# Moving eight modulation pairs of a diffusion backbone's opening from TensorE to VectorE, with split constants

## The reference

```python
ada_x = (silu(c) @ w_ada[l] + b_ada[l]).reshape(1, 1, 6, D)      # w_ada: (2, 1024, 6144)
ada_c = (silu(c_ctx) @ w_ada[l] + b_ada[l]).reshape(1, 1, 6, D)
h  = rms_norm(x, g1[l]) * (1 + ada_x[1]) + ada_x[0]
x  = x + ada_x[2] * mixer(h)          # l = 0: gated conv || spatial-gating MLP; l = 1: conformer || attention
h2 = rms_norm(x, g2[l]) * (1 + ada_x[4]) + ada_x[3]
x  = x + ada_x[5] * peer(h2)          # query, top-k search over keys, gather of 128 expert rows per token
```

## Time and profile before

| | us |
|---|---|
| median of 3 runs | 2404.74 (2398.95 to 2406.70) |
| profiled execution, its time | 2403.09 |
| profiled execution, its span | 2401.3 |

### The profile page before, as it was taken

The page is one execution under the profiler, slowest core; times in us unless marked ns, Lnnn a source line. Parts: engine busy times, 40 slices in busy tenths (PEclk is TensorE's granted clock), DMA queues, the critical chain, the costliest instruction groups (busy, mean ns, idle before and its releaser), DMA issues.

```text
span 2401.3 us, 24278 instructions
## 1 busy us (share of the span) xinstructions
PE 2093.0 (87%) x7016; PEld 1120.0 (47%) x7016; DVE 1550.1 (65%) x3844; ACT 958.4 (40%) x2802; POOL 1017.8 (42%) x868
## 2 busy tenths in 40 slices
PE   6997998789999988988799899798799987777777
PEld 4775554345566534543355355335456532222222
DVE  1126658885765577778856866854665887666444
ACT  2113434454333444444454333534443444444333
POOL 0002444444334454444545444430233555566774
PEclk9999999999999999999999999998899999999999
DMA  9966999999999999999999999995599999999997
GB/s 405 414 228 275 383 418 421 421 422 416 414 398 400 410 422 420 421 421 421 419 421 419 415 409 420 408 334 227 201 379 387 415 421 422 421 421 421 422 419 318
DMA packets 132451, 939.44 MB, mean 391 GB/s; under 512 B 14704, under 2 KB 17776, under 8 KB 18672
## 3 DMA queue, kind: packets, MB, share of 16 engines
q0 software_dynamic: 110592, 805.36, 81.7%
q1 hardware_dynamic: 21744, 132.68, 13.7%
HBM read 936.93 MB, written 1.05 MB: 391 GB/s over the span
## 4 chain that ended last, share of the span: by engine, by line
PE 35%; DMA 20%; DVE 10%; issue 5%; POOL 5%; ACT 4%; POOLq 0%; SPq 0%; DVEq 0%; ACTq 0%
DMA uv<-uv_dram,stage_idx 20%; PE psum L868 20%; PE psum L682 7%; DVE uv L1449 5%; POOL uv L936 5%; PE psum L664 4%; PE psum L813 1%; ACT diag L1107 1%; ACT wv L1105 1%; ACT gel L1103 0%; PE psum L842 0%; DVE work L1413 0%; PE psum L608 0%; DMA wring<-ada_dram 0%; PE psum L775 0%
## 5 line engine op out<-in xcount | busy, mean ns | idle before, releaser
L868 PE MATMUL psum<-uv,diag 128*128 128x512 f32 x3072 | 1452.9, 613 | 245.0 <-ACT diag L1107 238.2
L936 POOL DMA_INDIRECT uv<-uv_dram,stage_idx x768 | 981.6, 1278 | 1067.2 <-PE psum L868 834.4
L1449 DVE CUSTOM_DVE_ANT_0 uv<-uv,h 128x1024 f32<-128x1024 f32 x768 | 933.0, 1226 | 462.5 <-DMA uv<-uv_dram,stage_idx 451.7
L868 PEld LDWEIGHTS psum<-uv,diag 128*128 128x128 f32 x3072 | 561.7, 193 | 1032.6 <-ACT diag L1107 515.5
L1103 ACT ACTIVATE gel<-dots 128x1 f32<-128x1 f32 x768 | 154.5, 201 | 933.9 <-DVE dots L1449 931.5
L1107 ACT ACTIVATE diag<-const,wv 128x128 f32<-128x128 f32 x768 | 308.4, 402 | 25.0
L682 PE MATMUL psum<-hT,wring 128*128 128x256 f32 (+1 forms) x1344 | 284.6, 366 | 1.5 <-ACT hT L977 1.5
L682 PEld LDWEIGHTS psum<-hT,wring 128*128 128x128 f32 x1344 | 242.7, 194 | 63.3 <-issue 35.4
L1105 ACT ACTIVATE wv<-gel,gw 128x1 f32<-128x1 f32 x768 | 226.2, 295 | 24.9
L922 POOL COPY stage_idx<-idx 128x8 uint32 (+1 forms) x96 | 36.1, 376 | 293.3 <-DVE idx L1421 292.7
L959 ACT ACTIVATE work<-psum 128x256 f32<-128x256 f32 (+2 forms) x122 | 48.7, 400 | 251.6 <-PE psum L682 195.4
(11 more groups left out here) (210 smaller groups left out, 1284.7 us busy)
## 6 DMA issues: line engine op xcount, KB each, us to landing
uv<-ada_dram SPq DMA_DIRECT2D x37, 1024.0 KB, 12.7
wring<-in_dram SPq DMA_DIRECT2D x25, 1024.0 KB, 9.1
wring<-wq_dram SPq DMA_DIRECT2D x24, 1024.0 KB, 11.6
uv<-uv_dram,stage_idx POOLq DMA_INDIRECT x768
wring<-ada_dram SPq DMA_DIRECT2D x11, 1024.0 KB, 7.0
uv<-in_dram SPq DMA_DIRECT2D x9, 1024.0 KB, 16.7
wring<-out_w_dram SPq DMA_DIRECT2D x5, 1024.0 KB, 8.9
wring<-out_dram SPq DMA_DIRECT2D x4, 1024.0 KB, 11.1
```

The lines of the kernel that those rows point to most:

```text
L868: last = mm(acc[:, b, :], diag[:, s % RING, :], uv[:, s % RING, D + 512 * b:D + 512 * (b + 1)], start=(c == 0), stop=(c == NSEL - 1))
L936: nc.gpsimd.indirect_dma_start(out=uv[:, s, :], out_offset=None, in_=tables[stage // 2], in_offset=bass.IndirectOffsetOnAxis(ap=stage_idx[ ...
L1449: v.tensor_tensor_reduce(out=uv[:, r, 0:D], in0=uv[:, r, 0:D], in1=h2[:, row_of[stage], t, :], scale=1.0, scalar=0.0, op0=ALU.mult, op1=AL ...
```

## The change

Eight of the pairs of the opening (10 and 11 of layer 0, 0 to 5 of layer 1) are no longer computed by TensorE. Their weights come transposed (`ada_t`: a block holds two chunks, 128 partitions x 2 x 1024), and VectorE multiplies each chunk by the row of silu(c) and by that of silu(c_ctx), with the sum written to `ada_c` (a new step `ada_row`, 32 of them, two instructions each), and adds the bias after each fourth. The c rows are the vectors repeated on all partitions (1.05 MB, a new transfer), put through Silu by ScalarE at the first `mods`. `ada_row` steps are dealt among the steps of `project_even`, `gate` and `out_rows`; then the eight pairs left on TensorE (4 to 9 of layer 0, 6 and 7 of layer 1) among all of these. The constants come in two transfers: 276 columns first, the rest ahead of block 9. The scaling of x stands ahead of the wait for the modulation. TensorE does 28 products of ones ahead of everything, 14 and 6 more ahead of pairs 2 and 3, whose results nobody reads. The v projection of a tile waits for that tile of hT alone. Blocks up to the last dealt step are 54 in both kernels.

```diff
+ADA_ROWS = ((0, 10, 12), (1, 0, 6))
-PARTS = [("ident", P), ("iota", TOPK), ("cos", TT * 32), ("sin", TT * 32), ("c", KC * 2), ("b_ada", 2 * 48),
+PARTS = [("ident", P), ("c", KC * 2), ("b_ada", 2 * 48), ("norm_g", 2 * 2 * KC), ("gather_sums", 4),
+         ("iota", TOPK), ("cos", TT * 32), ("sin", TT * 32), ...
+W_EARLY = AT["iota"][0]
...
-        0: ada(0, 0, 2) + rms(0)[:3] + ada(0, 2, 4) + [("mods", 0, 0)] + rms(0)[3:] + norm(0, 0)
-        + deal(project_even(0), ada(0, 4, 12) + ada(1, 0, 4)) + gate(0, 0) + deal(out_rows(0, 0), ada(1, 4, 8)) + [("mods", 0, 1)]
+        0: [("idle", 28)] + ada(0, 0, 2) + rms(0) + [("idle", 14)] + ada(0, 2, 3)[:1] + [("idle", 6)] + ada(0, 2, 4)[1:] + [("mods", 0, 0)]
+        + norm(0, 0)
+        + deal(deal(project_even(0) + gate(0, 0) + out_rows(0, 0), [s for layer, first, last in ADA_ROWS for s in ada_rows_of(layer, first, last)]),
+               ada(0, 4, 10) + ada(1, 6, 8)) + [("mods", 0, 1)]
...
+            def idle(n_products):
+                for _ in range(n_products):
+                    mm(psum[:, 7, 0:P], ones[:, :], ones[:, :], start=True, stop=True)
...
             def v_project(stage, b, t):
-                wait_hT()
+                wait_hT(("hT", t))
...
-            sp.dma_start(const[:, :], A["const"]).then_inc(const_loaded, 16)
+            sp.dma_start(const[:, 0:W_EARLY], A["const"][:, 0:W_EARLY]).then_inc(const_loaded, 16)
...
+                if n == 9:
+                    sp.dma_start(const[:, W_EARLY:], A["const"][:, W_EARLY:]).then_inc(tables_loaded, 16)
+                if n == 9:
+                    sp.dma_start(c_rows[:, :, :], A["c_rows"]).then_inc(c_rows_loaded, 16)
...
             def mods(stage, which):                                   # ScalarE
-                n.up("mods")
+                if n.up("mods") == 1:
+                    act.wait_ge(c_rows_loaded, 16)
+                    f(c_rows, c_rows, ACT.Silu).then_inc(c_rows_ready, 1)
...
+            def ada_row(layer, chunk):                                # VectorE
+                i = n.up("ada_row") - 1
+                k = row_blocks[i // 2]
+                if i == 0:
+                    dve.wait_ge(c_rows_ready, 1)
+                dve.wait_ge(w_landed[w_slot[k]], landed[k])
+                if i:
+                    dve.wait_ge(row_sums, 2 * i)
+                w = w_home(k).rearrange("p (c d) -> p c d", c=2)[:, chunk % 2, :]
+                for j in range(2):
+                    v.tensor_tensor_reduce(out=row_tmp[:, j, :], in0=w, in1=c_rows[:, j, :], scale=1.0, scalar=0.0, op0=ALU.mult,
+                                           op1=ALU.add, accum_out=ada_c[:, layer, chunk, j:j + 1]).then_inc(row_sums, 1)
+                if chunk % 4 == 3:
+                    dve.wait_ge(row_sums, 2 * i + 2)
+                    pair = ada_c[:, layer, chunk - 3:chunk + 1, :]
+                    bias = C("b_ada", 2, 48)[:, layer, chunk - 3:chunk + 1].unsqueeze(2).to_broadcast([P, 4, 2])
+                    v.tensor_tensor(pair, pair, bias, ALU.add).then_inc(row_pairs, 1)
```

More of the change, by code:

```diff
@@ L97, in ada, with ada_rows_of @@
     return out + [("ada_turn", layer, last - 1)]
+def ada_rows_of(layer, first, last):
+    return [("ada_row", layer, chunk) for chunk in range(4 * first, 4 * last)]
 def gate(stage, which):
@@ L266, in weight_blocks @@
             uses = [(("ada", args[0], 2 * args[1] + j), ("ada", args[0], 2 * args[1] + j)) for j in range(2)]
+        elif name == "ada_row":
+            uses = [(("ada_row", args[0], args[1] // 2), ("ada_t", args[0], args[1] // 2))]
         elif name == "out_half":
@@ L438, in build @@
         row_of = (0, 1, 1)
+        c_rows = h2[:, 0, :, :]
+        row_tmp = h2[:, 1, :, :]
         kept_sc = vx[:, :, :].rearrange("p a (b c) -> p (a b) c", c=2 * PK).rearrange("p h (q k) -> p h q k", q=2)
@@ L462, in build @@
         const_loaded, x_loaded, ctx_loaded = sem("const_loaded"), sem("x_loaded"), sem("ctx_loaded")
-        constants_set = sem("constants_set")
+        tables_loaded, constants_set = sem("tables_loaded"), sem("constants_set")
         w_landed = [sem(f"w_landed{i}") for i in range(WRING + RING)]
@@ L470, in build @@
         dve_chain = sem("dve_chain")
+        c_rows_loaded, c_rows_ready, row_sums, row_pairs = (sem(s) for s in ("c_rows_loaded", "c_rows_ready", "row_sums", "row_pairs"))
         silu_ready, mods_ready, gdiag_ready = sem("silu_ready"), sem("mods_ready"), sem("gdiag_ready")
@@ L502, in build @@
         left = [{w_slot[k] - WRING: k for k in range(len(blocks)) if w_slot[k] >= WRING and in_gap[k] == g} for g in (False, True)]
+        landed = [16 * w_slot[:k + 1].count(w_slot[k]) for k in range(len(blocks))]
+        row_blocks = [k for k in range(len(blocks)) if blocks[k][0] == "ada_t"]
         def w_home(k):
@@ L577, in _ @@
         def _(pe):
-            n = Tally()
+            n = Tally(block=0)
             to_act, to_dve = act_banks(), dve_banks()
@@ L584, in weights @@
             def weights(what):
+                while n["block"] in row_blocks:
+                    n.up("block")
                 k = n.up("block") - 1
-                pe.wait_ge(w_landed[w_slot[k]], 16 * n.up(("w_slot", w_slot[k])))
+                pe.wait_ge(w_landed[w_slot[k]], landed[k])
                 held[what] = (k, w_home(k))
@@ L627, in ada_turn @@
                 taken["ada", layer, pair] = (act_took, to_act.n)
+            def ada_row(layer, chunk):
+                if chunk % 2:
+                    done = n.up("row_block")
+                    multiplied[row_blocks[done - 1]] = (row_sums, 4 * done)
+                if chunk % 4 == 3:
+                    taken["ada", layer, chunk // 4] = (row_pairs, n.up("row_pair"))
             def gate(stage, which, half):
@@ L637, in gate, with turn_rows @@
                 taken["gate", stage, which] = (act_took, to_act.n)
-            def turn_rows(*_):
+            def turn_rows(*args):
                 k = n.up("xn_ready")
@@ L649, in turn_rows, with wait_hT @@
                     banks.fill(last)
[L650 to L655, removed]
+                n["hT"] = n["hT", args[-1]] = (to_act.n, to_dve.n)
+            def wait_hT(of="hT"):
+                pe.wait_ge(act_took, n[of][0])
+                pe.wait_ge(dve_took, n[of][1])
             def token_major(banks, src, what, new, done):
@@ L848, in score @@
                     taken["scores", k, t] = (act_took, to_act.n)
-            steps = {"ada": ada_pair, "ada_turn": ada_turn, "gate": gate, "norm": turn_rows, "norm_ctx": turn_rows,
+            steps = {"idle": idle, "ada": ada_pair, "ada_turn": ada_turn, "ada_row": ada_row, "gate": gate, "norm": turn_rows, "norm_ctx": turn_rows,
                      "v_rows": v_project, "u_cols": noted("u_cols"), "ah_cols": noted("ah_cols"), "cg_cols": noted("cg_cols"),
@@ L874, in _ @@
             pe.wait_ge(constants_set, 1)
-            pe.wait_ge(const_loaded, 16)
             walk(steps, nothing, add_values, nothing)
@@ L1041, in conv_out_step @@
             def conv_out_step(stage):
+                act.wait_ge(tables_loaded, 16)
                 act.wait_ge(cn_ready, 1)
@@ L1197, in v_scale @@
                 invert(rr_v[:, :], "v")
+                if stage == 0:
+                    dve.wait_ge(tables_loaded, 16)
                 for t in range(TT):
@@ L1433, in find @@
                         dve.wait_ge(sc_used, k)
-            steps = {"mods": mods, "gate_diag": gate_diag, "rms_sum": rms_sum,
+            steps = {"mods": mods, "ada_row": ada_row, "gate_diag": gate_diag, "rms_sum": rms_sum,
                      "rms_root": rms_root, "rms_scale": rms_scale, "norm": lambda stage, which, t: modulate(hT[:, :, t * P:(t + 1) * P], stage, which),
@@ L1525 @@
         "ada": np.stack([in_columns(w_ada[i]) for i in range(2)]),
+        "ada_t": np.stack([w_ada[i].T.reshape(-1, 2, P, D).transpose(0, 2, 1, 3).reshape(-1, P, 2 * D) for i in range(2)]),
+        "c_rows": rows_(np.stack([c[0], c_ctx])).reshape(P, 2, D),
         "in": np.stack([in_columns(w_in[i]) for i in range(2)]),
```

7 lines of the change are left out of this document (5 added, 2 removed).

## The result

| | median us | runs | range |
|---|---|---|---|
| before | 2406.45 | 5 | 2398.95 to 2408.06 |
| after | 2390.24 | 5 | 2384.97 to 2394.42 |

The ratio of the runs' times is 0.9941 with a 95% interval of 0.9926 to 0.9956; on 2406.45 us that is 14.2 us faster (10.6 to 17.8). The two medians themselves lie 16.2 us apart. The forecast was 2391, in a range of 2382 to 2401.

What follows compares the result with a forecast made beforehand. TensorE bounds the opening before, VectorE much of it after: sum of squares at 163.4 instead of 176.57 gains 13.2 us, transposes 0.6, sum 13.8; 2403.1 - 13.8 = 2389.3, plus 1.6 for the median, taken as 2391, range 2382 to 2401.

Steps and rivals of the forecast that it cites:

- Where the gain comes from: Opening up to the first gather: pairs moved off TensorE make VectorE the bound there; 13.8 us gained in all.
- the first rival: Dealt steps of the opening: VectorE does not become the bound, blocks and TensorE set the end; 2385 us, chance 0.10.
- Transfers: Block landings in the opening: fourth pair 25.9 us, c rows 33.2, block 23 at 74.4, block 53 at 149.4.
- Silu: ScalarE ahead of its half of hT: one Silu over 2048 values of the c rows, 1.9 us, done at 35.1.
- first projection: Start of the opening: begins at 36.7 us instead of 38.48, behind the c rows' Silu and tile 0 of hT.
- VectorE's stretch: From its third spatial step to the second gate's diagonals VectorE never waits: 51.5 us, from 88.1 to 139.6.
- TensorE's waits: In that VectorE stretch TensorE waits some 7 us for unemptied banks and the diagonals, first at about 115.
- Clock: TensorE pauses before the ab steps and at both gates; 2 us added for lower clock, sum of squares at 163.4.
- First gather: End of the opening: first gather near 186 us instead of 199.39, 13.8 us gained and carried to the end.
- The unread products: 48 at the start, in pauses before pairs land; at worst the last six cost a microsecond, hidden by the c rows.
- the line of landings: Transfers of the opening: each lands at 3.10 us + bytes/0.4195 MB per us, 2.50 us a block.
- The slower rival: TensorE from about 115 us to the last projection: clock stays low between bank waits; 2416 us, chance 0.06.

Runs made afterwards that it cites:

- the third reduce: Changed kernel with a useless third multiply-reduce in each of the 32 row steps; first gather at 212.0 us against 188.9, 23.1 later.
- e5_silu_late: Changed kernel with ScalarE's wait for the c rows and their Silu moved behind its half of hT; first gather 188.1 us against 188.9.
- e7_rows: Changed kernel with only the eight pairs on VectorE, the start as before the change; first gather 188.4 us, ratio 0.9938 (0.9921 to 0.9954).
- e10_warm_half: Changed kernel plus 9, 7, 7 and 6 unread products in TensorE's four pauses at gates and close; first gather 184.3 us against 188.9.
- e11_row17: Changed kernel with the one row step between the two sets of gate diagonals moved behind them; first gather 188.9 us, as without the move.

## Why the prediction was right

Point by point, by the walk of the prediction:

- **Where the gain comes from: right.** The rows alone reach the first gather of the whole change, the third reduce costs 23 us, and VectorE is busy 49.24 of 51.00 us. That excludes the first rival.
- **Transfers: the shape right, the first term mis-sized.** The small first transfer was to bring the fourth pair from 28.16 to 25.9; it came at 27.43, released by its block. From there on all landings are 1.4 to 1.6 us late (c rows 34.6 for 33.2, block 23 at 76.0 for 74.4). Of the 2.2 us that 0.93 MB fewer ahead of that pair were to bring, 0.7 came. The DMA engines had hardly moved less. When the fourth pair started they had moved 10.46 MB, 0.9 MB more than the queue held up to that pair; before, it was 10.91 MB, 0.4 MB more. The 0.5 MB of later transfers that ran ahead are, by an estimate at the line's 0.4195 MB per us, 1.2 us, most of the 1.5. On SP the issues of the second part of the constants and of the c rows took 2.07 and 1.80 us and not some 0.4 each; both were out by 11.2, 23 us before the c rows landed.
- **Silu 1.91 us** for 1.9, that is 0.87 more than the Square of half its width and so a fixed share of 0.17 by these two, for 0.2; **first projection** 37.95 for 36.7, by the same lateness. The half clock behind TensorE's pause came too, 0.50 and 0.65 in the slices from 38 to 42, 1.7 us for about 2. Both were absorbed as said (`e5_silu_late`, `e7_rows`).
- **VectorE's stretch: right.** It begins at 90.66 for 88.1, and lasts to 140.9, 50.3 us for 51.5. Row steps are 2.30 to 2.41 where another instruction follows (114.76 to 117.06, 88.05 to 90.46 with the bias addition's wait) and 2.52 where the next row step does (85.53 to 88.05). The second gate starts at 141.00 for 139.6.
- **TensorE's waits: the size right, the place partly wrong.** Some 7 us of waits were forecast, for banks from about 115 on and for the diagonals; they are 6.3. But only one of them is for a bank (0.66 us before 117.81), 1.3 are for a block, and 4.3 stand at the two gates. The pause before the ab steps did not come.
- **Clock: the mechanism right, half the size.** The 2 us in the sum stand for one pause, and no run shows that term; the slices of the kernel before give (0.20 + 0.50 + 0.15) x 2 = 1.7 us of work lost behind its gates. Measured against `e10_warm_half` it is 2.9 us at the second gate and 1.7 in the close, which I had left out. The sum of squares comes at 165.50 for 163.4: 1.4 of that is the second gate's later start, the rest the clock's. In the close the transposes follow the sum of squares after 2.7 us (165.50 to 168.19) instead of 3.85, 1.2 earlier where I had said 0.6, and the low takes 1.7 back: 23.4 us where it took 22.8.
- **First gather** 188.9 for some 186: a gain of 10.5 for 13.8. The timed 14.2 us are closer to the forecast than the mechanism was: the terms above make 10.5, at the lower end of the interval. That the median of 2390.24 falls on the forecast 2391 within a microsecond is in part luck; with the 3.3 us that the prediction had too much, the same sum gives about 2394.
- **The unread products** were worth nothing where the change puts them, as said; their size was not worked out there. The 28 take 9.33 us and end at 10.6, some two microseconds behind the first pair's landing by the line of landings, so the first pair had to wait for them; the second still waits for its block, until 14.00, so nothing behind it moved. The last six took 1.60 us, and behind them TensorE still waited 1.50 for the fourth pair's block.
- **The slower rival: not met, and hardly put to the test.** TensorE's clock did not stay low for tens of microseconds: it is at 0.99 from 90 to 141. But the bank waits from which the rival starts were not there either, but for the one of 0.66 us. That one and the block wait of 1.29 us left the clock at 1.00. The pauses of 2.4 and 1.9 us at the gates brought it down behind the second in the kernel after, and behind the first already in `e11_row17` (0.54 from 138 to 140), so the length of a single pause does not say whether the clock falls. With one bank wait in 51 us the trace does not show what a series of them does to the clock.

What stays open: whether the 6.6 us of spread between tiles 4 and 5 are the clock's, what makes up the timed gain beyond 10.5 us, why later transfers ran ahead of the fourth pair's blocks behind a small first transfer, and what decides whether a pause of some 2 us at the gates is followed by the lower clock.

## What to carry to other kernels

Before you speed up the start of a pipeline, ask which transfer the next bound waits for: here 4 us of earlier start were given back at one block, and gains that were real alone did not add. When work moves to an idle engine, walk the list of steps in order and not only the sums; what stands between two hand-overs (one row step or two between the gate's diagonals) cost 2.6 us at the second gate and made a forecast gain a loss of 2.0. The pauses of 2.4 and 1.9 us at the gates cost TensorE 4.3 us here and the lower clock behind the second of them and in the close another 4.6, while waits of 1.3 and 0.7 us left the clock at 1.00; unread products that end inside the pause brought the first gather 4.6 us forward here, in one execution each, and twice as many brought nothing.

## What was not expected of the hardware

An fp32 product of 128x128 by 128 columns took 0.23 us at the upper clock level (36 records in 4.1 us for 18 products), two records for each. The column of the granted clock can stand at 1.00 over the first products of an execution although they take twice as long: in the kernel before, the first pair took 3.64 us and 1.93 in the kernel after, behind unread products, and the column shows 1.00 for both. A slice of the kernel before:

```profile
12.00:14.00 2.00, 2.00 (x24) 1.00 1.04 438
```

So for the first products the duration is to be believed and not the column. And a stretch of some 455 us whose instructions are the same in thirteen kernels varied by 6.6 us, 0.3% of the whole time, as much as many an edit is worth.
